# A two-block network on one core: input loaded first with idle products meanwhile, the last unit by token halves, and column sums of the modulation by transposes and GpSimd

## What is computed

```python
shift, scale, gate = split(silu(c) @ wm + bm, 3)                     # wm: 2048 x 6144
shift_c, scale_c = split(silu(c_ctx) @ wm[:, :4096] + bm[:4096], 2)
hx = rmsnorm(h, norm_g) * (1 + scale) + shift
hc = rmsnorm(ctx, norm_g) * (1 + scale_c) + shift_c
...                                     # projections, two attentions
h = h + gate * (concat(oa, ob) @ w_out)
return rmsnorm(h, final_g)              # 256 x 2048
```

## Time and profile before

| | us |
|---|---|
| median of 3 runs | 1993.85 |
| range of the runs | 1993.22 to 1994.78 |
| profiled execution, its own time | 1996.16 |
| its span in the trace | 1994.3 |
| PE busy, DVE busy, ACT busy, POOL busy | 1931.2, 1368.3, 959.8, 264.1 |
| granted TensorE clock, mean | 0.992 |

### The profile page before, as it was taken

How to read it: one execution, slowest core, us unless ns; L and a number is a source line. 1 busy time by engine, 2 the same in 40 slices (tenths; PEclk the granted TensorE clock), 3 DMA queues, 4 the chain that set the end, 5 groups by cost and what they waited for, 6 DMA issues and landing times.

```text
span 1994.3 us, 29135 instructions
## 1 busy us (share of the span) xinstructions
PE 1931.2 (97%) x11830; PEld 1701.5 (85%) x11830; DVE 1368.3 (69%) x1875; ACT 959.8 (48%) x1396; POOL 264.1 (13%) x436
## 2 busy tenths in 40 slices
PE   5999989999999999999999999999999999999997
PEld 5988989877888898988888788989898998988885
DVE  4677676665888878888877648656455567666674
ACT  5565656564533333344444455544333355545543
POOL 1027061623111111111111100100000000011000
PEclk9999999999999999999999999999999999999998
DMA  6554454544688878787787866755656544454563
GB/s 210 154 159 149 127 157 119 160 137 146 208 288 268 268 261 265 232 261 239 268 280 254 287 219 204 238 184 190 188 169 197 154 136 144 132 164 151 181 215 124
DMA packets 184837, 393.25 MB, mean 197 GB/s; under 512 B 12600, under 2 KB 12896, under 8 KB 183424
## 3 DMA queue, kind: packets, MB, share of 16 engines
q1 hardware_dynamic: 166240, 321.95, 49.7%
q0 software_dynamic: 17600, 67.78, 11.2%
q10 hardware_dynamic: 864, 1.67, 0.2%
HBM read 387.13 MB, written 4.23 MB: 196 GB/s over the span
## 4 chain that ended last, share of the span: by engine, by line
PE 80%; DVE 7%; POOL 4%; ACT 4%; issue 3%; DMA 1%; SPq 0%; ACTq 0%; DVEq 0%; POOLq 0%
PE GB L1998 46%; PE GB L2002 24%; POOL TB L1022 2%; DVE WL L1946 2%; POOL XB L1025 2%; ACT WH L1942 1%; PE SB L382 1%; PE SB L1638 1%; PE SB L1350 1%; DVE macc L1332 1%; PE SB L1739 1%; PE SB L1630 1%; PE SB L1746 1%; DMA wm<-in_w_mod 1%; DMA xin<-in_x 1%
## 5 line engine op out<-in xcount | busy, mean ns | idle before, releaser
L1946 DVE TENSOR_TENSOR WL<-raw,WH 128x1024 fp32r<-128x1024 f32 x608 | 733.7, 1230 | 263.2 <-ACT WH L1942 261.7
L1942 ACT ACTIVATE WH<-raw 128x1024 fp32r<-128x1024 f32 x608 | 625.0, 1056 | 357.7 <-PE GB L1998 230.7
L1998 PE MATMUL GB<-WH,uH 128*128 128x512 f32 x896 | 283.5, 398 | 2.1 <-DVE WL L1946 2.0
L1998 PE MATMUL GB<-WH,uL 128*128 128x512 f32 x896 | 278.0, 392 | 0.0
L1998 PE MATMUL GB<-WL,uH 128*128 128x512 f32 x896 | 277.9, 392 | 0.0
L2002 PE MATMUL GB<-uH,WH 128*128 128x256 f32 x1280 | 215.1, 291 | 5.2 <-DVE WL L1946 5.2
L1332 DVE SCALAR_TENSOR_TENSOR macc<-wm,csil,macc 128x512 f32<-128x512 f32 x300 | 209.2, 745 | 10.6 <-DMA wm<-in_w_mod 9.4
L2002 PE MATMUL GB<-uL,WH 128*128 128x256 f32 x1280 | 207.3, 285 | 0.0
L2002 PE MATMUL GB<-uH,WL 128*128 128x256 f32 x1280 | 207.0, 284 | 0.0
L1998 PEld LDWEIGHTS GB<-WL,uH 128*128 128x128 f32 x896 | 169.4, 189 | 35.9
L1998 PEld LDWEIGHTS GB<-WH,uL 128*128 128x128 f32 x896 | 169.0, 189 | 36.0
(11 more groups left out here) (391 smaller groups left out, 2190.6 us busy)
## 6 DMA issues: line engine op xcount, KB each, us to landing
raw<-in_w_in SPq DMA_DIRECT2D x512, 512.0 KB, 4.5
wm<-in_w_mod POOLq DMA_DIRECT2D x96, 512.0 KB, 5.8
raw<-in_w_out SPq DMA_DIRECT2D x96, 512.0 KB, 5.3
xin<-in_x SPq DMA_DIRECT2D x4, 512.0 KB, 6.7
E<-decay_rows POOLq DMA_DIRECT2D x4, 512.0 KB, 5.5
hres<-in_x POOLq DMA_DIRECT2D x1, 2048.0 KB, 10.6
cin<-in_ctx POOLq DMA_DIRECT2D x1, 2048.0 KB, 8.9
h_spill<-hres POOLq DMA_DIRECT2D x2, 1024.0 KB, 5.1
```

The costliest lines, as they stand in the source:

```text
L1942: e.activation(WH[s % NH][:, :, :], raw[s % NR][:, :, :], ACT.Copy).then_inc(*wh.inc("WH", s))
L1946: e.tensor_tensor(WL[s % NH][:, :, :], raw[s % NR][:, :, :], f32(WH[s % NH][:, :, :]), sub).then_inc(*wl.inc("WL", s))
L1998: m = e.matmul(banks[j][:, :], x[:, c, 128 * j:128 * j + 128], w[:, k, :], start=first, stop=last, skip_group_check=True)
```

## The change

Start: `vcol` goes to SP's queue behind `xin`; `wsm`, `rb` and POOL's constants are issued by POOL only when the third `raw` tile has landed; `wsL` is cleared at once. PE runs 30 matmuls of `ones` (`busy_pe`) whose result nothing reads. The Newton step has one instruction less, `xin` is scaled in parts of 512, 512 and 1024 columns (`scaled_act`, `scaled_dve`), the first split of a weight tile is ahead of the scaling on ACT and behind its first two parts on DVE, and two pairs of transposes instead of three are ahead of slot 0.

Modulation: DVE transposes `macc` in 32 x 32 blocks into `macT`, POOL halves it five times by additions, which leaves 16 columns for each vector and group in `msum`, and after the last group one matmul with a 0/1 matrix `fold` sums the four quarters of the partitions; eight small DVE additions at slot 346 write all of `modc`.

End: the 8 slots of the last unit are run for the first half of the tokens, then for the second half. Three more split buffers (`WX`) and a new `place` keep all 8 split tiles, and `split_until` lets the splits of the last slots run up to two slots further ahead. Each half has its own norm; the second is worked in pieces of 256 columns, and four DMAs of other sizes store.

```diff
-    steps("u", -1, 3, 100)
-    steps("u", 0, 5)
+    steps("u", -1, 2, 100)
+    steps("u", 0, 6)
...
+        def busy_pe(e):
+            for said, n in ((init.at("ones"), 15), ((x_in[2], 16), 5), ((x_in[3], 16), 6), (nx_dve.at("ss"), 4)):
+                e.wait_ge(*said)
+                for _ in range(n):
+                    e.matmul(SB[3][:, 0:128], ones[:, :], ones[:, :], start=True, stop=True, skip_group_check=True)
...
         def modulate_pool(e):
...
+                e.wait_ge(*mod_dve.at(f"{g}.t"))
+                t = macT[:, 0:heads_of(g), :].rearrange("p v (j r) -> p v j r", r=32)
+                for r in (16, 8, 4, 2, 1):
+                    if r < 16:
+                        e.wait_ge(*mod_pool.at(f"r{2 * r}", g))
+                    o = t[:, :, :, 0:r] if r > 1 else msum[:, 0:heads_of(g), 16 * g:16 * g + 16].unsqueeze(3)
+                    e.tensor_tensor(o, t[:, :, :, 0:r], t[:, :, :, r:2 * r], add).then_inc(*mod_pool.inc(f"r{r}", g))
                 yield
...
-                e.wait_ge(*mod_pe.at("s", g))
+                e.wait_ge(*mod_used(8 * g + 7))
+                if g:
+                    e.wait_ge(*mod_pool.at("r1", g - 1))
                 for v in range(heads_of(g)):
-                    c = (0, 48)[v] + 4 * g
-                    e.tensor_tensor(modc[:, c:c + 4], SB[0][:, 4 * v:4 * v + 4], vcol[:, BM + 4 * g:BM + 4 * g + 4],
-                                    add).then_inc(*mod_dve.inc(f"{g}.c{v}"))
+                    w = e.transpose(macT[:, v, :], macc[:, v, :])
+                w.then_inc(*mod_dve.inc(f"{g}.t"))
...
+            e.matmul(SB[0][:, 0:320], fold[:, :], msum[:, :, :].rearrange("p v j -> p (v j)")[:, 0:320], start=True, stop=True,
+                     skip_group_check=True).then_inc(*mod_pe.inc("s"))
...
+        def place(s):
+            if s < NS - 6:
+                return WH[s % NH], WL[s % NH]
+            if s < NS - 3:
+                return WX[s - (NS - 6)][:, 0], WX[s - (NS - 6)][:, 1]
+            return WH[(s - 8) % NH], WL[(s - 8) % NH]
...
+        def split_until(s):
+            return 1 if s < 0 else min(NS, s + min(AHEAD, s + 1) + 1 + min(2, max(0, s - (NS - 11))))
...
+            if unit.mode == "tok":
+                m = tokens_pe(e, unit, s, banks, (0,) if last_unit else (0, 1))
...
+            if s == NS - 1:
+                for i in range(8):
+                    m = tokens_pe(e, unit, NS - 8 + i, banks, (1,))
+                m.then_inc(*last_pe.inc("mm"))
```

More of the change, by code:

```diff
@@ L142, in timetable @@
     for g in range(12):
-        for i in range(8):
-            steps("mod", 128 + 18 * g + 2 * i, 1)
-        steps("mod", 128 + 18 * g + 17, 1)
+        at("mod", 128 + 18 * g, (0, 2, 4, 6, 8, 10, 12, 14, 17))
+    at("mod", 128 + 18 * 12, (1, 2))
     steps("mlrow", end("mlk", 0), 1)
@@ L1924, in last_dve @@
[L1924 to L1935 removed]
+            for i in range(2) if n < 3 else (0,):
+                out_sum_dve(e, n, i, banks)
@@ L1992, in product_pe @@
             for k in range(2):
                 H, L, c = moving(unit, 2 * i + k)
-                for n, (x, w) in enumerate(((H, WH[h]), (L, WH[h]), (H, WL[h]))):
-                    first, last = i == 0 and k == 0 and n == 0, i == 7 and k == 1 and n == 2
-                    if unit.mode == "tok":
-                        for j in range(2):
-                            m = e.matmul(banks[j][:, :], x[:, c, 128 * j:128 * j + 128], w[:, k, :], start=first, stop=last,
-                                         skip_group_check=True)
-                    else:
-                        for j in range(4):
-                            m = e.matmul(half(banks[j // 2], j % 2), w[:, k, 128 * j:128 * j + 128], x[:, c, :],
-                                         start=first and j % 2 == 0, stop=last, skip_group_check=True)
@@ L2004, in product_pe, with channels_pe @@
-            m.then_inc(*slot.inc("mm", s))
+                for n, (x, w) in enumerate(((H, wh_), (L, wh_), (H, wl_))):
+                    for j in halves:
+                        m = e.matmul(banks[j][:, :], x[:, c, 128 * j:128 * j + 128], w[:, k, :],
+                                     start=i == 0 and k == 0 and n == 0, stop=i == 7 and k == 1 and n == 2,
+                                     skip_group_check=True)
+            return m
+        def channels_pe(e, unit, s, banks):
+            i, (wh_, wl_) = SLOTS[s][1], place(s)
+            for k in range(2):
+                H, L, c = moving(unit, 2 * i + k)
+                for n, (x, w) in enumerate(((H, wh_), (L, wh_), (H, wl_))):
+                    for j in range(4):
+                        m = e.matmul(half(banks[j // 2], j % 2), w[:, k, 128 * j:128 * j + 128], x[:, c, :],
+                                     start=i == 0 and k == 0 and n == 0 and j % 2 == 0, stop=i == 7 and k == 1 and n == 2,
+                                     skip_group_check=True)
+            return m
@@ L2210, in _constants @@
     nmask = np.where((k >= c0) & (k < c0 + 16), f(0), f(NEG)).astype(f)
-    return dict(c_ident=ident, c_mask0=mask0, c_unit=unit, c_perm=perm, c_cos=cosT, c_sin=sinT, c_nmask=nmask)
+    return dict(c_ident=ident, c_mask0=mask0, c_unit=unit, c_perm=perm, c_fold=fold, c_cos=cosT, c_sin=sinT, c_nmask=nmask)
 def kernel(**inputs):
```

270 lines of the change are left out of this document (162 added, 108 removed).

## The result

| | before | after |
|---|---|---|
| median, us | 1993.53 (1993.17 to 1994.78, 4 runs) | 1966.12 (1964.33 to 1967.35, 4 runs) |
| ratio to before, 95% interval | | 0.9859 (0.9848 to 0.9871) |
| profiled execution: its own time, span | 1996.16, 1994.3 | 1964.33, 1962.5 |

What follows compares the result with a forecast made beforehand. PE, busy 97% of the span, was taken as the bound. Terms of -12.7 (start), -10.5 (modulation) and -4.3 (end) made -27.5 us, from the median 1993.85 to 1966.4; range 1957.5 to 1977.

Steps and rivals of the forecast that it cites:

- Start, -12.7: Start: earlier x, slot 0 from 14.2 to 17.1 at 2.4 GHz, one more transpose pair; -12.7 us (bounds -8.5 and -13.5).
- the `uL` behind it: Start: the last step on PE before slot 0, after two matmul pairs and one `uH` pair; 0.5 us.
- the clock is not held: Rival, start: idle products end too early, slot 0 at 1.2 GHz again, start -9, total 1970; chance 0.12.
- Modulation, -10.5: Modulation: PE saves 16.5 us of column sums and waits 6 us anew; -10.5 us (bounds -16.5 and -0.5).
- The stalls: Modulation: PE's new waits, as the `wm` load stands behind GpSimd's additions; 6 us over twelve groups, bounds 0 and 16.
- The hold: Modulation: time five GpSimd additions hold VectorE through the shared port; 1.9 us per group of two vectors.
- the lock for the whole instruction: Rival, modulation: first to start fully blocks the other; hold 3.0 us a group, 6 us more, 1972; chance 0.12.
- GpSimd becomes the bound: Rival, modulation: additions take 6.0 us a group, 48 us more, 2014; decides from about 4.7 us; chance 0.03.
- each microsecond counts twice: Step of that rival: longer additions cost as a hold and as a later load, 6 us more in eight groups.
- End, -4.3: End: last DMA issued 5.7 us after PE's end instead of 9.5; -4.3 us (bounds -3 and -5).
- the landing and the closing: End: time from the issue of the last DMA to the span's end; 5.0 us of the 5.3 before.
- All that follows is bound by PE and moves up with it: Behind the start: everything later shifts by the start's gain; slots 6 to 128 were forecast at 0 change.

Runs made afterwards that it cites:

- start_dma: Kernel after with the start transfers of before (vcol, rb, wsm on ACT's queue, constants at once on POOL's) and wsL cleared late; 1973.04 us.
- mod_back: Kernel after with the modulation of before: column sums by eight matmuls a group on PE, no transposes, no GpSimd additions; 1974.68 us.
- adds_twice: Kernel after with each of GpSimd's modulation additions done twice (sums come out wrong); 2021.80 us.
- end_back: Kernel after with the end of before: last unit not split in token halves, splits not moved ahead, one norm for both halves; 1972.58 us.
- warm: Kernel after with w_mod load ahead of additions, hres load cut into eight (1959.68 us), plus idle products at start and behind ScalarE's y5 wait; 1966.98 us.
- warm2: `warm` with the idle products of the quads (14, 7, 14 and 12) issued ahead of both waits, ScalarE's y5 too; 1954.33 us.

## Why the prediction was right, and where it was not

**Start, -12.7.** Measured -10.0 in the profiled pair; `start_dma` gives 6.9 back. The sum itself has two slips: 12.1 and 0.6, 0.9 and 0.5 make 14.1, not 14.2, and 30.5 less 17.1 less 0.44 makes 13.0, not 12.7. Two sizes were off. x's last quarter came at 9.27, not at 8.5 (0.8). Slot 0 started at 15.51 instead of 14.2: the other 0.5 is "the `uL` behind it", for which I took 0.5, while two `uL` of the first pair stand before slot 0, from 14.57 to 15.5. That slot 0 runs at 2.4 GHz was wrong in this execution (1.5 us), right in five of seven with this start. The rival "the clock is not held" came true in the profiled execution and not in five of the seven; it is a matter of the execution. `wsL`, the order of the loads and the extra transpose pair (0.44) were right.

**Modulation, -10.5.** Measured -9.4. PE's saving, 16.5 in the forecast, is 17.3: 17.9 less the one matmul of 0.58. The stalls, forecast at 6 (0 to 16), are 7.9 or so, but not by my working, so the good size of this term is luck. The additions took 4.9 a group of two vectors (2.175 + 0.920 + 0.672 + 0.651 + 0.500, means in the trace), not 3.0; part of this is queueing behind VectorE. The hold, forecast at 1.9, was right: in group 0 the five VectorE instructions beside the additions took 1.54, 0.96, 0.95, 0.78 and 1.27, where the same ones take 0.48, 0.48, 0.75, 0.75 and 1.22 in the mean in `mod_back`, which makes 1.8. The load landed 4.2 after its issue, not 5.8, and VectorE waited 1.96, not 4.6. So the split of slot 152, where I saw the stall, was ready 1.3 us before its use, and PE waited where VectorE is full with the mLSTM stage, which I had not looked at.

**The rivals on GpSimd.** The Trainium skill's rule of the lock for the whole instruction ("SBUF — State Buffer", "SBUF: two separate sides") fits the first addition: it takes 2.175 in the mean, in group 0 some 1.0 of it until the split ends at 551.49, the rest near the 1.26 of the earlier trace rows, and the `macc` instruction beside it takes 1.1 longer. It does not give the sum: all five together cost VectorE the 1.8 of above in group 0, not 3.0, and the last two of them 0.1. "GpSimd becomes the bound" had the right chain, which `adds_twice` shows, but not its size. Its point of decision, 4.7 us of additions a group, was wrong: at 4.9 the kernel gained all the same. And the 2021.8 of `adds_twice` came at 9.5 us of additions a group, where the rival had 2014 at 6.0 already. The step of this rival that failed is "each microsecond counts twice", which left out that VectorE has other work to do meanwhile.

**End, -4.3.** Measured -4.9 (`end_back`) to -5.4. The chain after PE was right: the scaling starts 4.0 after PE's end, and the last three stores are issued from 4.6 to 5.5 after it, where I had the last at 5.7. My own items (2.0, 0.6, 1.6 and 0.9) make only 5.1, and 5.7 and 5.0 make 10.7, not the tail of 10.5 on which the -4.3 rests. The term that was mis-sized is the landing and the closing, 5.0: from the issue of the last store (1958.6) to the span's end it is 3.9. No run shows why.

**What I left out.** "All that follows is bound by PE and moves up with it" is not true of the 17 us at 1.2 GHz between slots 6 and 128 nor of slot 334. The table shows the first: 452.4 with none, 456.3 to 456.8 with 10.2, 457.2 to 459.2 with 13.7, 459.4 to 460.9 with 17.1 and 463.8 with 23.9; `warm`, whose idle products stand in the way, is the exception. Nine of these kernels, after among them, have the same code there and lie between 456.3 and 460.1, a tenth, `adds_twice`, at 463.8. So the 3.7 of the profiled pair is no more than two executions of one kernel can differ by, and I put it down to where they fell. The clock makes only part of it: PE waits 20.0 instead of 22.4, and 1.6 of this is one wait, in slot 73, that takes 2.2 in the kernel after, 3.8 before and 4.3 in `adds_twice`. The medians, which average over this, show 27.4; undoing one part costs 8.6 (modulation), 6.5 (end) and 6.9 (loads and `wsL`), 22.0 together. The rest of the start, above all the scaling of `xin` in parts and the new order around it, was not undone by itself: from x's last quarter to slot 0 the time fell from 12.5 to 6.2, and the variance makes 1.5 of that. Whether each stretch at 1.2 GHz is set off by the wait right before it was not tried one by one.

## What to carry to other kernels

When a PE-bound kernel has a few waits of 2 to 4 us, their price can be the wait and time at 1.2 GHz around it. Look at the clock column in each such stretch, and put idle products ahead of every wait of that place, not between two. A load that stands behind new work on GpSimd's queue can cost more than the work (here 3.8 of PE's time against 1.8): issue it first, and split large loads that are needed late. Compare slot by slot before believing that a total confirms a sum.

## What the runs showed that I had not expected

- 10 to 17 us at 1.2 GHz in 450, beside waits of 2 to 4 us, go with 4 to 8 us more than in `warm2`, which has none. That they also make the spread between executions is not shown: the runs of `warm2` lie within 0.7 us, but those of `warm`, with 13.7 us at 1.2 GHz, within 0.5.
- With 30 idle products of 128 columns that end 1 us before the first transposes, slot 0 ran at 2.4 GHz in five executions of seven.
- With one transfer of 2 MB PE stalls 0.5 to 4.1 us at slot 334, differently in each kernel; with the transfer cut into eight it does not.
- Doubling 4.9 us of GpSimd additions a group costs 55.7 us in all, part of it through the clock; leaving most of them out gains 6.0.
- Five GpSimd additions held VectorE for 1.8 us in group 0, and nearly all of that came from the first three.
